# A hybrid decoder step: order of split and eviction in two projections, and the banks of the down products

## What is computed

```python
xn = rmsnorm(x, norm_mix);  proj = xn @ w_in            # 1024 x 3328
z  = p_cur + (p_shift - p_cur) * mu_shift               # token shift of the first 14 column tiles
r, k, v, ... = split(z);  kk = k * k_k;  kk = kk / norm(kk)
...                                                     # delta-rule scan, gated conv, w_out
q  = (rmsnorm(x, norm_x) @ wq);  x = x + attention(q, mem_k, mem_v) @ wo
up = rmsnorm(x, norm_ffn) @ w_up                        # 1024 x 5632
u, g = split(causal_dwconv3(up));  x = x + (silu(g) * u) @ w_down   # 2816 x 1024
```

## Time and profile before

| | |
|---|---|
| median of 3 runs | 4683.84 us (4681.19 to 4686.91) |
| the profiled execution | 4681.24 us |
| its span | 4679.5 us |
| mean granted clock of TensorE | 0.937 of full |
| TensorE matmul busy | 4164.8 us, 89% |
| VectorE / ScalarE / GpSimd busy | 2313.4 / 1501.5 / 1411.3 us |

### The profile page before, as it was taken

How to read it: one execution, slowest core, us unless ns; L and a number is a source line. 1 busy time by engine, 2 the same in 40 slices (tenths; PEclk the granted TensorE clock), 3 DMA queues, 4 the chain that set the end, 5 groups by cost and what they waited for, 6 DMA issues and landing times.

```text
span 4679.5 us, 58079 instructions
## 1 busy us (share of the span) xinstructions
PE 4164.8 (89%) x21561; PEld 3439.6 (74%) x21561; DVE 2313.4 (49%) x4929; ACT 1501.5 (32%) x2926; POOL 1411.3 (30%) x1226
## 2 busy tenths in 40 slices
PE   3699988998899889997999889996999696989996
PEld 3579866886689767885799657885889473878885
DVE  1256635555266535555365445544356535255554
ACT  1343333333433333333433333333333221032222
POOL 6242022443231124442431224441331020123331
PEclk9899999999899999997999989997999797689997
DMA  2320122332310213332200322332200112212221
GB/s 69 130 81 1 50 68 72 99 96 76 104 50 1 82 41 104 95 99 86 86 24 1 104 67 82 99 95 72 68 28 1 54 59 87 89 59 73 73 72 56
DMA packets 455040, 322.17 MB, mean 69 GB/s; under 512 B 18012, under 2 KB 420262, under 8 KB 453070
## 3 DMA queue, kind: packets, MB, share of 16 engines
q1 hardware_dynamic: 454758, 318.45, 22.2%
HBM read 296.99 MB, written 21.61 MB: 68 GB/s over the span
## 4 chain that ended last, share of the span: by engine, by line
PE 76%; DVE 13%; issue 4%; ACT 3%; POOL 2%; DMA 1%; DVEq 0%; ACTq 0%; SPq 0%; POOLq 0%
PE psum L577 74%; DVE xlo L1314 2%; PE psum L581 1%; DVE xT L1314 1%; DVE shifted L1314 1%; POOL wlo L482 1%; DVE ws L1314 1%; POOL stage L415 1%; DVE S L1513 1%; DVE kkn_y L1317 1%; DVE xT L1317 1%; ACT L983 0%; DVE stage L1314 0%; DMA out_y_prompt<-zr 0%; ACT stage L983 0%
## 5 line engine op out<-in xcount | busy, mean ns | idle before, releaser
L482 POOL TENSOR_TENSOR wlo<-wraw,whi 128x1024 fp32r<-128x1024 f32 x480 | 1149.2, 2395 | 2688.7 <-ACT whi L983 2688.0
L577 PE MATMUL psum<-xhi,whi 128*128 128x512 f32 (+1 forms) x3136 | 1247.9, 398 | 73.2 <-DVE xlo L1314 54.6
L577 PE MATMUL psum<-xlo,whi 128*128 128x512 f32 (+1 forms) x3136 | 1219.8, 389 | 0.0
L577 PE MATMUL psum<-xhi,wlo 128*128 128x512 f32 (+1 forms) x3136 | 1219.5, 389 | 0.0
L983 ACT ACTIVATE whi<-wraw 128x1024 fp32r<-128x1024 f32 x480 | 507.2, 1057 | 1355.9 <-PE psum L577 1290.8
L577 PEld LDWEIGHTS psum<-xhi,whi 128*128 128x128 f32 x3136 | 597.1, 190 | 244.6 <-issue 60.5
L577 PEld LDWEIGHTS psum<-xhi,wlo 128*128 128x128 f32 x3136 | 597.0, 190 | 124.0
L577 PEld LDWEIGHTS psum<-xlo,whi 128*128 128x128 f32 x3136 | 598.5, 191 | 114.5 <-issue 2.2
L1314 DVE TENSOR_TENSOR xT<-xT,psum 128x512 f32<-128x512 f32 x416 | 285.9, 687 | 216.6 <-PE psum L577 162.7
L1617 DVE TENSOR_SCALAR zr<-zr,fcw 128x512 f32<-128x512 f32 x176 | 91.8, 522 | 604.8 <-POOL fcarry L519 604.1
L577 PE MATMUL psum<-ws 128*128 128x64 f32 (+1 forms) x2560 | 337.9, 276 | 0.0
(11 more groups left out here) (292 smaller groups left out, 5461.3 us busy)
## 6 DMA issues: line engine op xcount, KB each, us to landing
wraw<-in_w_up SPq DMA_DIRECT2D x176, 512.0 KB, 3.8
wraw<-in_w_in SPq DMA_DIRECT2D x104, 512.0 KB, 3.9
wraw<-in_w_down SPq DMA_DIRECT2D x88, 512.0 KB, 3.5
wraw<-in_w_out SPq DMA_DIRECT2D x32, 512.0 KB, 4.0
wraw<-in_wq SPq DMA_DIRECT2D x32, 512.0 KB, 4.0
wraw<-in_wo SPq DMA_DIRECT2D x32, 512.0 KB, 4.0
kkn_y<-in_x_prompt SPq DMA_DIRECT2D x4, 2048.0 KB, 9.4
xT_scratch<-xT SPq DMA_DIRECT2D x4, 2048.0 KB, 7.6
```

Of the source, the lines that this page charges most:

```text
L482: return e.tensor_tensor(wlo[i][:, :, :], wraw[i][:, :, :], whi[i][:, :, :].bitcast(F32), ALU.subtract).then_inc(lo_ready[i], 1)
L577: return e.matmul(out, lhsT, rhs, start=start, stop=stop)
```

## The change

Three edits:

- `down_bank`: in the three blocks without samples, the eight down products go through banks 0, 1, 4, 5, 0, 1, 4, 5 in place of banks 0 to 7. In the last block they keep banks 0 to 3, twice.
- In projection, the 14 shifted tiles: ScalarE splits the weights' high half ahead of waiting for `shifted` to be free and of its three evicting instructions, in place of behind them.
- Query projection: ScalarE splits the weights' high half ahead of the eviction.

```diff
         def down_bank(k, samples):
 
-            return k % 4 if samples else k
+            return k % 4 if samples else (0, 1, 4, 5)[k % 4]
...
                         e.wait_ge(slab_done[j], c(slab_done[j]))
+                        split_w(j)
                         e.wait_ge(shf_free[j], c(shf_free[j]))
                         act(shifted[:, j, 0:1], carry[:, bass.ds(m, 1)])
                         act(shifted[:, j, 1:TB + 1], psum[:, j, :], scale=pcol("mu_shift", m)).then_inc(ach, 1)
                         e.wait_ge(ach, c(ach))
                         act(carry[:, bass.ds(m, 1)], shifted[:, j, TB:TB + 1]).then_inc(shf[j], 1)
-                        split_w(j)
...
                         e.wait_ge(slab_done[j], c(slab_done[j]))
+                        split_w(j)
                         act(q_sb[:, bass.ds(2 * i + j, 1), :].rearrange("p a t -> p (a t)"), psum[:, j, :]).then_inc(ach, 1)
                         e.wait_ge(ach, c(ach))
                         e.sem_inc(free[j], 1)
-                        split_w(j)
```

## The result

The changed kernel takes 4772.12 us, beside 4685.35 us before: a ratio of 1.019, 95% interval 1.017 to 1.021. (This is the median of three of its four runs. The fourth stood at 10678 us, as no other run of any kernel here did; with it the median would be 4774.99.) The direction was forecast and the size was not: 87 us more between the medians, where the forecast had 64 and the range ended at 4767. The profiled execution took 4771.21 us (before: 4681.24), so the two traces differ by 90.0 us, and that is the sum to be explained.

A forecast was written before the change was run, and what follows sets the result against it. TensorE alone was taken to bound the feed-forward part. Banks 62.4 us, query projection +3.8 and in projection -2.0 gave 64.2 us on the profiled 4681.24, or 4745.4; the forecast against the median was 4747, range 4729 to 4767.

The forecast's parts named there:

- The stall: Feed-forward, three blocks without samples: k = 4 waits for the first addition to free bank 0, 2.14 us each.
- the release: Time from the end of VectorE's addition to TensorE's start behind it: 0.12 us.
- the restart: The first matmul behind a wait takes longer to hand over to the second: 0.16 us more.
- The tenth group: Feed-forward group before down(10), where TensorE idles anyway: 1.3 us per block, between 0.8 and 2.1.
- the estimate of 1.7: Cost in us of the tenth group if the second hidden product waits for GpSimd's whole moved split.
- The clock: Rival: TensorE's clock falls at each of 30 idle stretches, 1.8 us each, 54 us in all, 4801 us; chance 0.07.
- Queries: End of the query projection: eighth eviction and first scores come 0.94 us later, 3.8 us over four blocks.
- Squares: End of the in projection: TensorE's wait for the last square goes, 0.66 us in each of three blocks, -2.0 us.
- Attention's clock: Attention stages, shifted in time, may lose or regain clock: -4 to +8 us, in the range only.
- The covered wait: Rival: something brings VectorE's addition forward, so k = 4 doesn't wait; 4679 us, chance 0.05.

The follow-up runs named there:

- e4_fill8: The changed kernel with eight unread matmuls into unused bank 7 ahead of the wait of k = 4, in the three blocks without samples: 4748.4 us, ratio 1.0134.
- e6_early: The changed kernel, banks 0, 1, 4, 5 kept, with VectorE's first two additions moved ahead of the fourth up tile's convolution: 4680.3 us, ratio 0.9991.
- e1_banks: The kernel before with only the down products' banks changed to 0, 1, 4, 5, both projections as before: 4770.3 us, ratio 1.0184.
- e2_proj: The kernel before with only the two projections' weight splits moved, down products through banks 0 to 7: 4686.9 us, ratio 1.0004.
- e7_far: The changed kernel with down products through banks 4, 5, 0, 1, 6, 7, 4, 5: 4683.9 us, ratio 1.0.
- e5_fill4: The changed kernel with four unread matmuls into unused bank 7 ahead of the wait of k = 4: 4754.4 us, ratio 1.0144.
- e3_six: The changed kernel with down products through banks 0, 1, 4, 5, 6, 7, 0, 1: 4741.8 us, ratio 1.0119.

## Why the prediction was right and wrong, point by point

**The stall: right in place, number and size, the last with some luck.** 30 waits; 2.14 us forecast, 2.18 measured; the addition ends 1.86 us behind the time at which k = 4 wants to start, as read from the earlier trace rows. Two small terms were off and nearly cancel: the release took 0.20 us where the sum had 0.12, and the restart cost 0.08 us at the second matmul and 0.04 more behind it, where the sum had 0.16. The 0.16 was read from 1141.53 in the earlier trace rows, where TensorE ran at the lower clock.

**The tenth group: mis-sized.** Forecast 1.3 us, measured 1.7 in all three blocks (2.18 less the 0.48 won back), within the bounds. The eighth addition came 0.8 us later, as forecast. The two hidden products took 3.44 us where they took 2.42: the second of them ended only behind GpSimd's split (VectorE, then GpSimd):

```profile
1168.40 3.44 DVE L1314 TENSOR_TENSOR stage<-zr 128x512 f32<-128x512 f32 x2
1171.76 0.68 DVE L1314 TENSOR_TENSOR hlo<-stage,hhi 128x512 fp32r<-128x512 f32 x1
...
1168.69 2.60 POOL L482 TENSOR_TENSOR wlo<-wraw,whi 128x1024 fp32r<-128x1024 f32 x1 [3.85 <-ACT whi L983]
```

The Trainium skill, "GPSIMD Engine Reference", specifications, has such instructions contend with GpSimd; the estimate of 1.7 that the prediction set beside it is what was measured, and these rows agree with it.

**The clock: the step that failed.** The prediction had the price of a fall nearly right (1.8 us against 1.6 measured) and took its chance for all or nothing: 30 falls or none, 0.07 for the former, and neither the sum nor the range has anything between. The trace has 13, 20.7 us together. The argument was that 2.0 us of idle time lies below the 2.7 at which the clock had fallen in the earlier trace rows. In that row TensorE stayed idle while the clock fell, so it tells when the clock fell in that stretch, and not how much idle time suffices. Behind the stalls the clock falls after TensorE has restarted, 0.2 to 1.5 us later.

The trace of the kernel before held the case itself, and the prediction doesn't show it. At the start of the last block's feed-forward part TensorE is idle for 1.79 us; it was busy for the whole stretch before at the full clock (second line), and 0.6 us after the restart it is at the lower one (third line):

```profile
4175.66 0.25 PE L577 MATMUL psum<-xs,whi 128*128 128x32 f32 x1 [1.79 <-DVEq L1633]
...
4140.00:4173.80 33.80, 33.80 (x181) 28.73 (x179) 18.21 (x41) 10.07 (x14) 12.18 (x15) 1.00 0.23 64
...
4176.20:4179.80 3.60, 3.60 (x16) 3.41 (x16) 3.42 (x6) 0.00 (x0) 1.50 (x3) 0.51 0.31 95
```

Nor does a longer idle time always bring a fall. In the attention of block 0, in the same trace, one of 3.27 us has the full clock within it and behind it:

```profile
706.57 0.44 PE L581 MATMUL psum<-ident,zr 128*128 128x128 f32 x2 [3.27 <-DVE zr L1598]
...
703.30:706.50 3.20, 0.00 (x0) 0.00 (x0) 2.58 (x6) 1.39 (x4) 0.00 (x0) 1.00 0.00 0
706.50:709.00 2.50, 1.84 (x9) 1.40 (x10) 2.00 (x9) 1.63 (x5) 0.00 (x0) 1.00 0.03 7
```

So these rows left it open how many of the 30 stalls would have a fall, and the range should have held any number from 0 to 30; with half of them the forecast would have been 4774. The Trainium skill, "TensorE: Matmul & The Clock Gate", section on psum-queue depth-cycling, has the clock oscillate when TensorE idles briefly between groups as it cycles through PSUM banks. The prediction gave this little weight; the 13 stretches at 0.43 us a step, and `e4_fill8`, in which they are gone, agree with it.

**Queries: right at the wait, too much in the sum.** Forecast +0.94 us each, and the first scores come 0.91 us later in all four blocks. But twelve matmuls on TensorE had to wait anyway, and 0.35 us of it comes back there, so that four blocks pay 2.2 us and not 3.8. ScalarE starts the eviction 0.96 us behind the split's start:

```profile
671.51 1.06 ACT L983 ACTIVATE whi<-wraw 128x1024 fp32r<-128x1024 f32 x1 [3.90 <-PE psum L577]
672.47 0.58 ACT L983 ACTIVATE zr<-psum 128x512 f32<-128x512 f32 x1
...
673.27 1.53 PE L577 MATMUL psum<-ws,zr 128*128 128x256 f32 x6 [1.80 <-issue]
```

**Squares: right, by the mechanism named.** Forecast -0.66 us each, measured -0.78. The first multiplication takes 0.53 us in place of 2.38, and TensorE goes from the sixteenth tile to the sums without a wait:

```profile
272.24 0.53 DVE L1722 TENSOR_SCALAR kkn_y<-zr,par 128x512 f32<-128x512 f32 x1
...
276.03 2.50 DVE L1722 TENSOR_SCALAR kkn_y<-zr,par 128x512 f32<-128x512 f32 x1
```

```profile
279.40 0.39 PE L577 MATMUL psum<-xhi,wlo 128*128 128x512 f32 x1
279.63 0.59 PE L577 MATMUL psum<-ws,ones_bd 128*128 128x512 f32 x1
```

One multiplication, the fourth, now meets GpSimd in its turn, but early enough. Inside the projections nothing waits, as forecast.

**Attention's clock: in the range, at nothing in the sum.** In block 0 the changed kernel has a mean clock of 0.55 from 708 to 717 us, where the kernel before has 1.00 from 706 to 715, and loses 4.2 us; behind the queries of the last block it loses 2.7. The sum had nothing for either, and the range had 8. The other profiles don't settle whether the new order brings it. Block 0's attention has a slow stretch there, of 3 or 10 us, in all kernels with a projection changed but `e6_early`, and none in the kernel before and in `e1_banks`; yet `e2_proj`, with both projections changed, can't be told from the kernel before in its median.

**The covered wait** is what `e6_early` and `e7_far` show when it is made: 4680 and 4684 us, against the 4679 that the rival named. The forecast gave it 0.05, and rightly: nothing in the change itself brings the addition forward.

## What to carry to other kernels

When a buffer is shared by fewer users, write down for each of its uses when it is wanted and which instruction frees it, the next stage's first use included, and look where the freeing instruction stands in its engine's order: the engine can be half idle and still come to it too late. Moving that instruction into an idle gap ahead of a long piece of work was worth as much here as more buffers. And price a short wait on TensorE twice, once for its length and once for the clock behind it. Look in the trace that you have for the shortest idle stretch with a fall behind it, not only within it; where a row shows only that a longer wait let the clock fall, the shorter one is unknown, not safe.

## What the runs showed of the hardware

- Short idle stretches on TensorE between stretches of full work let the clock fall in some cases and not in others. By length, with the run: 0.9 us, none of 28, and 1.25 us, none of 2 (`e5_fill4`); 1.46 us, none of 24, and 1.8 us, one of 3 (`e3_six`); 1.9 us, 12 of 28, and 2.3 us, one of 2 (the change, and the same again in the banks alone). In the change and the banks alone the falls are one to three groups apart; what picks the stall stays open.
- Each of these falls in the change came after the restart, 0.2 to 1.5 us behind it, and cost 1.6 us: seven to nine steps at or near 0.43 us.
- Eight matmuls that nobody reads, put into the stall, made the kernel 24 us faster (4772.1 to 4748.4), and with four of them the profiled execution had no fall either.
